# Two transfers per cached page instead of three, rope keys taken from the page rows, and low parts exchanged between GpSimd and VectorE

## What is computed

```python
ckv = concatenate([cache_ckv_l[pages].reshape(past, KV_LORA), ckv_new])   # 2048 + 8 rows of 256
kpe = concatenate([cache_kpe_l[pages].reshape(past, QK_ROPE), kpe_new])   # the same rows, 32 values
k = build_keys(ckv, kpe, w_uk, k_head_norm)     # rmsnorm([W_uk c | kpe]) per head, 64 + 32 wide
s = einsum('qhd,khd->hqk', q, k) * SCALE        # 8 queries, 8 heads
p = softmax(masked s)
o_lat = einsum('hqk,kc->qhc', p, c_kv)          # values are taken in latent space
```

## Time and profile before

| | before |
|---|---|
| median of 3 runs (lowest, highest) | 1536.07 us (1535.14, 1537.04) |
| the profiled execution, its span | 1533.52 us, 1531.5 us |
| TensorE matmul, busy | 1491.3 us (97%) |
| VectorE, busy | 1067.9 us (70%) |
| ScalarE, busy | 655.5 us (43%) |
| GpSimd, busy | 454.3 us (30%) |
| DMA engines, mean busy share of SyncE's queue | 33.1% |

### The profile page before, as it was taken

The page is one execution under the profiler, slowest core; times in us unless marked ns, Lnnn a source line. Parts: engine busy times, 40 slices in busy tenths (PEclk is TensorE's granted clock), DMA queues, the critical chain, the costliest instruction groups (busy, mean ns, idle before and its releaser), DMA issues.

```text
span 1531.5 us, 31143 instructions
## 1 busy us (share of the span) xinstructions
PE 1491.3 (97%) x10771; PEld 1434.9 (94%) x10771; DVE 1067.9 (70%) x1738; ACT 655.5 (43%) x1215; POOL 454.3 (30%) x463
## 2 busy tenths in 40 slices
PE   8999999999999999999999888999999999999999
PEld 8999999999999999588888888888999999999999
DVE  7999898421269975865888788854759998985000
ACT  6444445322221242464666666642434444445111
POOL 4000002454465744320344333223551000005432
PEclk9999999999999999999999999999999999999999
DMA  6233234222333651003444443432222332332322
GB/s 176 70 103 103 82 97 116 78 83 75 82 83 100 83 116 47 13 4 99 129 127 129 124 125 111 128 106 72 83 83 56 109 97 85 106 92 81 91 77 82
DMA packets 245460, 141.69 MB, mean 93 GB/s; under 512 B 22705, under 2 KB 242290, under 8 KB 245362
## 3 DMA queue, kind: packets, MB, share of 16 engines
q1 hardware_dynamic: 244498, 139.97, 33.1%
q10 hardware_dynamic: 864, 0.48, 0.1%
HBM read 136.82 MB, written 3.58 MB: 92 GB/s over the span
## 4 chain that ended last, share of the span: by engine, by line
PE 52%; issue 24%; SPq 11%; POOL 7%; DVE 3%; ACT 1%; DMA 1%; POOLq 0%; DVEq 0%; ACTq 0%
PE ps L493 28%; PE ps L1522 14%; POOL w_lobuf L468 7%; SPq L726 3%; SPq L731 3%; SPq L742 3%; SPq L737 2%; PE ps L1861 2%; PE ps L1647 1%; PE ps L1701 1%; PE ps L1676 1%; PE ps L479 1%; PE ps L1691 1%; DMA w_rawbuf<-in_ffn_w_gu 1%; DVE cT_lo L2466 1%
## 5 line engine op out<-in xcount | busy, mean ns | idle before, releaser
L468 POOL TENSOR_TENSOR w_lobuf<-w_rawbuf,w_hibuf 128x256 fp32r<-128x256 f32 (+1 forms) x328 | 316.4, 996 | 801.4 <-ACT w_hibuf L461 801.3
L1522 PE MATMUL ps<-xs,w 128*128 128x288 f32 x3192 | 427.7, 296 | 0.8 <-DVE w L1984 0.8
L1522 PEld LDWEIGHTS ps<-xs,w 128*128 128x128 f32 x3192 | 426.8, 188 | 1.5 <-issue 1.5
L461 ACT ACTIVATE w_hibuf<-w_rawbuf 128x1024 fp32r<-128x1024 f32 (+1 forms) x89 | 104.4, 1173 | 353.3 <-PE ps L493 332.9
L2192 DVE SCALAR_TENSOR_TENSOR xT<-ps,xT 128x576 f32<-128x576 f32 x23 | 17.4, 756 | 202.4 <-PE ps L493 202.4
L1984 DVE TENSOR_TENSOR w<-w_raw,w 128x512 fp32r<-128x512 f32 x228 | 154.0, 690 | 0.3 <-ACT w L1029 0.2
L493 PE MATMUL ps<-a_hi,w_lobuf 128*128 128x288 f32 x682 | 147.5, 297 | 0.0
L493 PE MATMUL ps<-a_hi,w_hibuf 128*128 128x288 f32 x682 | 147.2, 296 | 0.0
L493 PE MATMUL ps<-x_hi,w_hibuf 128*128 128x288 f32 x656 | 142.2, 298 | 4.1 <-POOL w_lobuf L468 2.9
L493 PE MATMUL ps<-a_lo,w_hibuf 128*128 128x288 f32 x682 | 145.5, 294 | 0.0
L493 PE MATMUL ps<-x_lo,w_hibuf 128*128 128x288 f32 x656 | 140.8, 296 | 0.0
(11 more groups left out here) (335 smaller groups left out, 2602.6 us busy)
## 6 DMA issues: line engine op xcount, KB each, us to landing
w_raw<-in_ffn_w_gu SPq DMA_DIRECT2D x76, 256.0 KB, 2.9
up_rows<-in_ffn_w_gu SPq DMA_DIRECT2D x72, 256.0 KB, 3.2
c_nat<-in_pages_in SPq DMA_DIRECT2D x128, 144.0 KB, 2.2
c_ring<-in_pages_t SPq DMA_DIRECT2D x128, 128.0 KB, 2.1
w_rawbuf<-in_w_in SPq DMA_DIRECT2D x58, 256.0 KB, 3.2
w_rawbuf<-in_ffn_w_down SPq DMA_DIRECT2D x32, 384.0 KB, 4.0
w_rawbuf<-in_ffn_w_down SPq DMA_DIRECT2D x32, 320.0 KB, 3.4
w_rawbuf<-in_ffn_w_gu SPq DMA_DIRECT2D x24, 256.0 KB, 3.4
```

Source lines behind the costliest of these rows:

```text
L461: act.activation(w_hibuf[:, r % HIS, 0:size], w_rawbuf[:, r, 0:size], ACT.Copy).then_inc(w_hi_done, 1)
L468: ins = pool.tensor_tensor(w_lobuf[:, r, part], w_rawbuf[:, r, part], w_hibuf[:, r % HIS, part].bitcast(F32), ALU.subtract)
L1522: mm = pe.matmul(ps[:, seven_bank(f, slot), 0:HALF], m, xs[:, slot, n, k, :], start=k == 0 and j == 0, stop=k == KH - 1 and j == 2)
```

## The change

Each page gets two transfers instead of three. The rope keys are no longer loaded transposed: VectorE copies them for four pages out of the rows (`kpe_rows`), TensorE transposes them into a spare part of PSUM bank 6 after page 4g + 2, ScalarE copies the result to `kpeT` (`kpe_copy`), and the rope product after page 4g + 3 waits for that copy. SyncE works in pairs of pages instead of groups of four. From sequence 1 on, the low part of the transposed pages is made by GpSimd, and the low part of the probabilities by VectorE, at the start of pair 5. The values are taken ahead of page 11 and in the middle of page 14, the fold ahead of page 15; the high parts of the late pairs are made one page earlier.

```diff
+        kpe_rows = place("kpe_rows", [P, 4, DR], F32, ring_at + 8 * DK * P + 8192 + 8 * (SQ + KN + SQ))
...
-        kpe_in = [sem(f"kpe_in{g}") for g in range(2)]
...
-        SPLITS = PAIRS + 2
+        SPLITS = PAIRS
-        LATE_AT = 11
+        LATE_AT = 10
...
-            return r * SPLITS + (EARLY_PAIRS + 1 if j < EARLY_PAIRS else j + 3)
+            return r * SPLITS + (j + 1)
...
+        def pages_lo(eng, s, pp):
+            eng.wait_ge(ct_hi, s * PAIRS + (pp + 1))
+            eng.tensor_tensor(cT_lo[:, pp % 2, :], ring_pair(pp), cT_hi[:, pp % 2, :].bitcast(F32), ALU.subtract).then_inc(ct_lo, 1)
...
-            return 3 if at(s, g) == (0, 0) else 4 * g + 1
+            return 3 if at(s, g) == (0, 0) else 4 * g + 2
...
-            def load_ring(g, found):
-                for u, page in enumerate(found):
-                    sp.dma_start(c_ring[:, (4 * g + u + RING // 2) % RING, :], pages_t[ds(page, 1), :, :].rearrange("a p c -> (a p) c"))\
-                        .then_inc(ring_in[g % 2], 16)
-            def load_rows(b, g, found):
-                for u, page in enumerate(found):
-                    sp.dma_start(c_nat[:, b, 4 * g + u, :], pages_in[ds(page, 1), :, :].rearrange("a p c -> (a p) c")).then_inc(nat_in[b][g], 16)
-            def load_kpe(g, found):
-                for u, page in enumerate(found):
-                    sp.dma_start(kpeT[u * DR:(u + 1) * DR, g % 2, :], pages_k[ds(page, 1), :, :].rearrange("a d t -> (a d) t")).then_inc(kpe_in[g % 2], 16)
-            def load_pages(s, b, used=None):
-                for g in range(NP // 4):
-                    found = [page_of(s, 4 * g + u) for u in range(4)]
-                    sp.wait_ge(ct_lo, s * PAIRS + (2 * g - 2))
-                    load_ring(g, found)
-                    sp.wait_ge(pe_scored, s * (NP // 4) + (g - 1))
-                    load_kpe(g, found)
-                    if used is not None:
-                        sp.wait_ge(pages_used, used + 2 * (g + 1))
-                    load_rows(b, g, found)
+            def load_ring(pp, two):
+                for u, page in enumerate(two):
+                    sp.dma_start(c_ring[:, (2 * pp + u + RING // 2) % RING, :], pages_t[ds(page, 1), :, :].rearrange("a p c -> (a p) c"))\
+                        .then_inc(ring_in[pp % 2], 16)
+            def load_rows(b, pp, two):
+                for u, page in enumerate(two):
+                    sp.dma_start(c_nat[:, b, 2 * pp + u, :], pages_in[ds(page, 1), :, :].rearrange("a p c -> (a p) c")).then_inc(nat_in[b][pp // 2], 16)
+            def load_pair(s, b, pp, used=None):
+                two = [page_of(s, 2 * pp + u) for u in range(2)]
+                sp.wait_ge(ct_lo, s * PAIRS + (pp - 1))
+                load_ring(pp, two)
+                if used is not None:
+                    sp.wait_ge(pages_used, used + (pp + 1))
+                load_rows(b, pp, two)
             sp.wait_ge(rows_done, 2 * NT + PT_TILES)
-            found = [page_of(0, u) for u in range(4)]
-            load_ring(0, found)
-            load_kpe(0, found)
+            early = [[page_of(0, 2 * pp + u) for u in range(2)] for pp in range(2)]
+            for pp in range(2):
+                load_ring(pp, early[pp])
             sp.wait_ge(prep_q, 1)
-            load_rows(0, 0, found)
-            for g in (1, 2):
-                load_rows(0, g, [page_of(0, 4 * g + u) for u in range(4)])
+            for pp in range(2):
+                load_rows(0, pp, early[pp])
+            later = [[page_of(0, 2 * pp + u) for u in range(2)] for pp in range(2, 4)]
+            for pp in range(2, 4):
+                load_rows(0, pp, later[pp - 2])
             sp.wait_ge(prep_tr, 2)
             sp.wait_ge(uk_split, 1)
-            found = [page_of(0, 4 + u) for u in range(4)]
-            load_ring(1, found)
-            load_kpe(1, found)
-            load_rows(0, 3, [page_of(0, 12 + u) for u in range(4)])
-            for g in (2, 3):
-                found = [page_of(0, 4 * g + u) for u in range(4)]
-                sp.wait_ge(ct_lo, 2 * g - 2)
-                load_ring(g, found)
-                sp.wait_ge(pe_scored, g - 1)
-                load_kpe(g, found)
+            for pp in range(2, 4):
+                sp.wait_ge(ct_lo, pp - 1)
+                load_ring(pp, later[pp - 2])
+            for pp in range(4, PAIRS):
+                load_pair(0, 0, pp)
             sp.wait_ge(prep_mm, 2)
-            load_pages(1, 1)
+            for pp in range(PAIRS):
+                load_pair(1, 1, pp)
             with sp.Fori(1, NS // 2) as i:
                 for b in range(2):
-                    load_pages(i * 2 + b, b, i * (2 * PAIRS) + (EARLY_PAIRS + PAIRS * (b - 2)))
+                    for pp in range(PAIRS):
+                        load_pair(i * 2 + b, b, pp, i * (2 * PAIRS) + (EARLY_PAIRS + PAIRS * (b - 2)))
...
-            def probabilities_low(r, b, half):
-                t = slice(half * NP // 2, (half + 1) * NP // 2)
-                pool.wait_ge(p_done, exp_made(r, half))
-                ins = pool.tensor_tensor(p_two[:, t, 1, :], s_buf[:, b, t, :], p_two[:, t, 0, :].bitcast(F32), ALU.subtract)
-                if half:
-                    ins = pool.tensor_tensor(p_two[0:TS, NP, 1, :], s_buf[0:TS, b, NP, :], p_two[0:TS, NP, 0, :].bitcast(F32), ALU.subtract)
-                ins.then_inc(split_made, 1)
             def squares(s, b, uses, prev, nxt):
-                if prev and stacked(s):
-                    for j in range(EARLY_PAIRS):
-                        split_pair(s - 1, 1 - b, j)
-                    for half in range(2):
-                        probabilities_low(s - 1, 1 - b, half)
-                    for j in range(EARLY_PAIRS, PAIRS):
-                        split_pair(s - 1, 1 - b, j)
+                later = not (isinstance(s, int) and s == 0)
+                for pp in range(PAIRS):
+                    if later and pp < PAIRS - 1:
+                        pages_lo(pool, s, pp + 1)
+                    if prev and stacked(s):
+                        for j in ((), (), (0, 1), (2, 3), (), (4, 5), (6, 7), ())[pp]:
+                            split_pair(s - 1, 1 - b, j)
+                if not later:
+                    pool.wait_ge(ct_lo, PAIRS)
+                if nxt:
+                    pages_lo(pool, s, PAIRS)
                 if not nxt:
                     split_lo(pool, n_merge, n_merge % RAWS, KD * P)
                 for g in range(NP // 4):
                     pool.wait_ge(nat_in[b][g], uses * 64)
+                pool.wait_ge(kpe_row, s * 4 + 4)
...
-                act.wait_ge(ring_in[pp // 2 % 2], (s * 2 + (pp // 4 + 1)) * 64)
+                act.wait_ge(ring_in[pp % 2], (s * 4 + (pp // 2 + 1)) * 32)
...
+            def kpe_copy(s, g):
+                act.wait_ge(pe_tr, s * 4 + (g + 1))
+                if not (isinstance(s, int) and s == 0 and g < 2):
+                    act.wait_ge(pe_scored, s * 4 + (g - 1))
+                act.activation(kpeT[:, g % 2, :], ps[:, PEB, 4 * HQ:4 * HQ + P], ACT.Copy).then_inc(pe_copied, 1)
...
+                        if t == kpe_page(s, t // 4):
+                            kpe_copy(s, t // 4)
...
+                    pe.wait_ge(p_low, r + 1)
...
-            def kpe_scores(s, g):
-                pe.wait_ge(kpe_in[g % 2], (s * 2 + (g // 2 + 1)) * 64)
+            def kpe_transpose(s, b, g, uses):
+                pe.wait_ge(kpe_row, s * 4 + (g + 1))
                 if isinstance(s, int) and s == 0 and g == 0:
                     pe.wait_ge(prep_copied, 2)
-                else:
+                if not (isinstance(s, int) and s == 0 and g == 0):
                     pe.wait_ge(scores_read, s * 4 + g)
+                pe.transpose(ps[:, PEB, 4 * HQ:4 * HQ + P], kpe_rows[:, :, :].rearrange("p t d -> p (t d)"), ident[:, :])\
+                    .then_inc(pe_tr, 1)
+            def kpe_scores(s, g):
+                pe.wait_ge(pe_copied, s * 4 + (g + 1))
...
-                            for _ in range({12: 4, 15: 4}.get(t, 0)):
+                            for _ in range({11: 4, 15: 1}.get(t, 0)):
...
-                            if prev and k == 1 and t in ((7, 8, 15) if stacked(s) else (7, 8)):
+                            if prev and k == 1 and t in (7, 8):
                                 next(soft)
+                            if prev and stacked(s) and k == 1 and t == 14:
+                                for _ in range(EARLY_PAIRS):
...
+                        if t == kpe_page(s, g):
+                            kpe_transpose(s, b, g, uses)
...
+                    yield
...
+            def probabilities_low(r, b):
+                for half in range(2):
+                    t = slice(half * NP // 2, (half + 1) * NP // 2)
+                    dve.wait_ge(p_done, exp_made(r, half))
+                    dve.tensor_tensor(p_two[:, t, 1, :], s_buf[:, b, t, :], p_two[:, t, 0, :].bitcast(F32), ALU.subtract)
```

(15 more changed lines are left out.)

18 lines of the change are left out of this document (8 added, 10 removed).

## The result

The changed kernel takes 1570.05 us (median of 4 runs, 1568.18 to 1570.16) against 1535.61 us (4 runs, 1533.72 to 1537.04): the ratio is 1.0222, 95% interval 1.0204 to 1.0240. It is slower, as forecast, but by 34 us and not by 14, and it lies outside the range (1535 to 1561). Its profiled execution is 1569.98 us with a span of 1568.2 us, against 1531.5.

A forecast was written before the change was run, and what follows sets the result against it. Limits seen: SyncE's issue rate and ScalarE's fixed order of handoffs. Looped sequences +6.0, sequence 3 -1.0, sequence 5 +1.5, sequence 0 +1.0, sequence 7 +4.5, clock +2: 14 over the median 1536.07, so 1550; range 1535 to 1561.

The forecast's parts named there:

- SyncE's relief: Page stretch: 32 transfers per sequence instead of 48, a group about 7.4 us instead of 9.4, so the transfer limit goes.
- the waits at the rope product: After page 3, the rope product waits for ScalarE's late copy of the keys: +0.8 us per looped sequence.
- in sequence 7: Rope product of pages 8 to 11 starts 6.5 us late behind ScalarE's copy, TensorE idle some 5.5; sequence total +4.5 us.
- the denominators' wait: Sequence 7: the 3.11 us wait and 0.4 of restart come back, no longer behind a low part on VectorE.
- A: Rival, faster: SyncE was the limit and the copies are in time; -8.7 us, 1527; chance 0.17.
- B: Rival, about as before: loop costs as forecast, but ScalarE reaches sequence 7's copy in time; 1538; chance 0.13.
- D: Rival: the ring's shorter lead makes ScalarE, then TensorE, wait each pair; +24 us, 1560; chance 0.05.
- the clock: Half clock behind the page 11 wait in two of six sequences, 1.0 us each: +2 us, bounds 0 and 10.
- rival C: Slower still: the wait at page 11 drops the clock in all six sequences; +22 us, 1558; chance 0.15.
- the low probabilities (4): Page 11: values wait for all exponentials, then VectorE's low parts; TensorE stands 3.1 us, +1.1 us per looped sequence.
- the copy of the rows: After page 6, the transposition waits for VectorE's copy behind the sums: +0.3 us per sequence, the last group +0.1.
- 0.12 us for a transposition: TensorE's cost for one of the four added transpositions per sequence; two fall in other waits, two cost 0.25 us.

The follow-up runs named there:

- x1_lock: The changed kernel, with GpSimd held off the low part of pair 6 until VectorE's low probabilities are done; 1559.03 us, ratio to before 1.0160.
- x2_half: The changed kernel, values of pairs 0 to 3 waiting only for the first half of VectorE's low probabilities, the others for the second; 1550.08 us.
- y2_rows: The changed kernel, with VectorE's copy of the rope rows placed between the sums of a pair's two pages; 1564.00 us, ratio to before 1.0178.
- w1_before_s7: The kernel before, with ScalarE's split of the first merge weight one pair later in the last sequence; 1531.38 us, ratio 0.9961.
- b2_exch: The kernel before with only the exchange: GpSimd makes the pages' low parts, VectorE those of the probabilities; 1534.79 us, ratio 0.9991.
- w3_low_early: The changed kernel with per-half value counts, later merge-weight split, row copy between the sums, first low-part pass ahead of the second sum; 1532.30 us.

## Why the prediction was right and wrong

**Right.** Slower, with its reasons: SyncE's relief does not reach the end; the waits at the rope product (0.35 us after page 3), at page 11 and in sequence 7 (5.28 us, foreseen as 5.5) have the releasers that I named; the fold waits for nothing, though in sequence 5 the transposition behind it waits 1.35 us for VectorE; the denominators' wait is gone. Rivals A and B are out by the time and by the wait in sequence 7, D because the ring holds no pair. No low part of GpSimd holds a pair by more than 0.65 us.

**Wrong, first term: the clock.** I gave it 2 us for two of six sequences with 10 as the upper bound; it took 13.6, of which 11.8 cost time. That was rival C, at 0.15: the clock fell at page 11 in all six. The step that failed is the choice of "two of six" at 1.0 us each. The number of falls had no reason from a row: in the page stretch before, both waits above 2 us, the 2.08 of sequence 3 and the 3.11 of sequence 7, had lost their clock. The price was read off one window of 2 us; the half clock behind the 2.08 lasts from 852.7 to 856.2, which is 1.7 us lost, as the windows on either side of that of the earlier trace rows show:

```profile
852.00:854.00 2.00, 2.00 (x13) 1.91 (x12) 0.77 (x3) 1.16 (x3) 0.00 (x0) 0.67 0.39 124
856.00:858.00 2.00, 2.00 (x16) 2.00 (x16) 1.80 (x4) 0.71 (x2) 0.00 (x0) 0.98 0.63 193
```

This term and the next are not independent. In x1_lock, where TensorE stands 3.0 us at page 11, the transposition included, about the 3.1 that I had forecast, the clock falls there in sequences 1, 3 and 4 only. In the windows that begin in sequences 4 to 6 a second drop came on top (3.3 to 3.6 us lost in each).

**Wrong, second term: the low probabilities (4).** "0.15 for the new rows" measured 1.28 us beside GpSimd and 0.21 without it (x1_lock): 1.1 us a sequence, 6.5 in all. The prediction had weighed the rule for it, in the Trainium skill ("SBUF — State Buffer", section "SBUF: two separate sides"): the shared port is locked for a whole instruction, and the other engine blocks fully. The trace agrees (1.28 us beside a pass of GpSimd of 1.26), and more sharply than at the place where I priced it (page 14, up to 0.5 us): a short instruction there pays the whole length of the long one. I had applied it only to the engine that was new to the work, not to the pass with the least slack. Even so the pass was on the path only because one semaphore now covers it (x2_half); that belongs in part 4 of the sum and was not there.

**The rest of the sum holds, in total.** For sequence 2, +4.2 us less 1.7 of clock and 1.1 of the blocked pass leaves +1.4, where 1.55 was summed. Adding 12.0, 11.8 and 6.5 gives 30.3 of the 32.8 us of the stretch. Inside it two errors partly cancel: sequence 6 cost more (waits of 2.25 and 2.40 us for the copy of the rows, which stands behind VectorE's norm passes and which I had priced at 0.3), sequence 7 less than 4.5 on this cut. The 0.12 us for a transposition is right as such: in sequence 0 four pages take 6.75 us before, 6.87 in y2_rows, where the copy comes early, but 7.16 in the changed kernel, where it comes just late. So sequence 0 cost 2.1 and not 1.0.

**Not foreseen: 3.0 us of start-up.** In the profiled executions of the other seventeen kernels the first rope product starts between 721.7 and 726.3 us; that of before, at 720.5, is the earliest of all, and w1_before_s7, whose start-up code is that of before, is the latest. It is scatter of that stretch, and I do not count it to the change. It goes with the clock: ahead of the first product 3.4 us of granted clock are lost in that of before, 6.8 in the changed kernel and 10.2 in w1_before_s7. What decides whether the clock falls there was not settled.

**What stays open.** Why x1_lock, with waits of 1.5 and 1.0 to 1.2 us, kept its clock at page 11 in sequence 2 and lost it in 1, 3 and 4 was not separated. No run holds the rule by which the clock falls. That the price of 0.8 for the rope product hides GpSimd's late low part is argued from b2_exch (1.39 us ahead of page 4 there; 0.27 here, which ScalarE's square ends), not tried by itself.

## What to carry to other kernels

When one semaphore takes the place of several counts, ask for every waiter which of the merged producers it needed, and price the latest; here splitting the count again returned 20 of the 34 us. Where a wait is added on TensorE, price the clock behind it at every place that repeats it, by the whole length of a half clock in the trace and not by one window of it. And a limit that is not the last to end returns nothing when lifted (SyncE at 11% of the chain), but comes back when the others have gone: the full change with its waits repaired (w3_low_early, 0.9976) beats the kernel before, though moving one line in the kernel before (w1_before_s7, 0.9961) does as much. Since w3_low_early holds that edit too, the change itself gave nothing measurable beyond it.
